# Reading the moving operand of 256-token products by turns from two halves, with u, hid and ry begun at a multiple of 1024 bytes

## The reference

```python
def _swiglu(xn, w_in, w_out):
    a, b = jnp.split(xn @ w_in, 2, axis=-1)
    return (jax.nn.silu(a) * b) @ w_out
```

## Time and profile before

| | |
|---|---|
| median of 3 runs | 2204.13 us (2203.73 to 2204.4) |
| the profiled execution's own time | 2210.91 us |
| its span, from first to last instruction | 2209.1 us |
| TensorE matmuls, busy | 2198.0 us (99%), 18114 instructions |
| TensorE weight loads, busy | 2180.8 us (99%), 18114 instructions |
| VectorE, ScalarE, GpSimd busy | 73%, 58%, 13% |
| granted TensorE clock | full in all 40 slices (2.4 GHz) |
| DMA engines | 52.2% on the queue of the weights, 174 GB/s read and written over the span |

### The profile page before, as it was taken

How to read it: one execution, slowest core, us unless ns; L and a number is a source line. 1 busy time by engine, 2 the same in 40 slices (tenths; PEclk the granted TensorE clock), 3 DMA queues, 4 the chain that set the end, 5 groups by cost and what they waited for, 6 DMA issues and landing times.

```text
span 2209.1 us, 48942 instructions
## 1 busy us (share of the span) xinstructions
PE 2198.0 (99%) x18114; PEld 2180.8 (99%) x18114; DVE 1602.4 (73%) x2450; ACT 1276.6 (58%) x1988; POOL 282.1 (13%) x328
## 2 busy tenths in 40 slices
PE   8999999999999999999999999999999999999999
PEld 8999999999999999999999999999999999999999
DVE  6655997665566579887768767888768766777775
ACT  6444786544444368766546646876556645565662
POOL 0001661100100136220020012010010010101000
PEclk9999999999999999999999999999999999999999
DMA  6555435555455544455555555355556645445553
GB/s 229 174 188 165 159 122 170 167 171 195 155 173 183 179 161 144 144 185 186 190 169 193 195 183 163 124 178 194 195 181 200 219 162 177 161 162 194 188 200 124
DMA packets 100408, 386.68 MB, mean 175 GB/s; under 512 B 11312, under 2 KB 12464, under 8 KB 100304
## 3 DMA queue, kind: packets, MB, share of 16 engines
q1 hardware_dynamic: 99648, 383.89, 52.2%
q0 software_dynamic: 368, 1.26, 0.2%
q10 hardware_dynamic: 288, 0.12, 0.0%
HBM read 384.18 MB, written 1.05 MB: 174 GB/s over the span
## 4 chain that ended last, share of the span: by engine, by line
PE 98%; ACT 1%; DVE 1%; issue 0%; DMA 0%; ACTq 0%
PE bank L387 16%; PE bank L389 15%; PE bank L388 15%; PE bank L395 15%; PE bank L396 14%; PE bank L397 14%; PE bank L759 1%; PE bank L1049 1%; PE bank L1050 1%; PE bank L1051 1%; PE bank L1096 0%; PE bank L709 0%; PE bank L740 0%; PE bank L940 0%; PE bank L943 0%; PE bank L942 0%
## 5 line engine op out<-in xcount | busy, mean ns | idle before, releaser
L412 DVE TENSOR_TENSOR wlo<-raw,whi 128x1024 fp32r<-128x1024 f32 (+1 forms) x677 | 893.3, 1322 | 177.8 <-ACT whi L405 165.4
L405 ACT ACTIVATE whi<-raw 128x1024 fp32r<-128x1024 f32 (+1 forms) x677 | 745.5, 1112 | 164.5 <-PE bank L389 117.2
L387 PE MATMUL bank<-u,whi 128*128 128x272 f32 (+1 forms) x1888 | 549.0, 291 | 7.1 <-DVE u L450 7.1
L389 PE MATMUL bank<-u,wlo 128*128 128x272 f32 (+1 forms) x1888 | 543.7, 288 | 0.0
L388 PE MATMUL bank<-u,whi 128*128 128x272 f32 (+1 forms) x1888 | 541.9, 287 | 0.0
L395 PE MATMUL bank<-u,whi 128*128 128x256 f32 x1888 | 529.2, 280 | 0.2
L397 PE MATMUL bank<-u,wlo 128*128 128x256 f32 x1888 | 527.4, 279 | 0.0
L396 PE MATMUL bank<-u,whi 128*128 128x256 f32 x1888 | 527.4, 279 | 0.0
L387 PEld LDWEIGHTS bank<-u,whi 128*128 128x128 f32 x1888 | 356.9, 189 | 8.0 <-DVE wlo L412 7.3
L388 PEld LDWEIGHTS bank<-u,whi 128*128 128x128 f32 x1888 | 357.0, 189 | 0.9 <-issue 0.2
L397 PEld LDWEIGHTS bank<-u,wlo 128*128 128x128 f32 x1888 | 357.6, 189 | 0.0
(11 more groups left out here) (332 smaller groups left out, 3448.8 us busy)
## 6 DMA issues: line engine op xcount, KB each, us to landing
raw<-w SPq DMA_DIRECT2D x552, 512.0 KB, 3.4
raw<-w SPq DMA_DIRECT2D x128, 704.0 KB, 4.1
h<-xT SPq DMA_DIRECT2D x4, 272.0 KB, 4.9
outT<-h SPq DMA_DIRECT2D x8, 128.0 KB, 4.7
consts<-cst POOLq DMA_DIRECT2D x1, 576.0 KB, 4.6
dist<-cst POOLq DMA_DIRECT2D x1, 192.0 KB, 2.7
rdist<-cst POOLq DMA_DIRECT2D x1, 192.0 KB, 3.0
sgain<-small POOLq DMA_DIRECT2D x1, 145.5 KB, 4.8
```

What stands on the lines that cost most here:

```text
L387: pe.matmul(out, w_h, x_hi, start=first, stop=False)
L389: return pe.matmul(out, w_l, x_hi, start=False, stop=last)
L405: act.activation(whi[:, n % RING, 0:COLS[n]], raw[:, n % RING, 0:COLS[n]], ACT.Copy).then_inc(hi_ready, 1)
L412: dve.tensor_tensor(wlo[:, n % RING, 0:COLS[n]], raw[:, n % RING, 0:COLS[n]], whi[:, n % RING, 0:COLS[n]], ALU.subtract).then_inc(lo_ready, 1)
```

## The change

Two things. `U_PAD`, `HID_PAD` and `RY_PAD` are each 16 elements (64 bytes) less, so that tiles of 256 tokens begin at a multiple of 1024 bytes in u, hid and ry. And the three matmuls of `split_products` no longer walk their 256 columns from first to last: both the moving operand and the output are given as a pattern of 8 x 2 x 16, in which 16 columns of the first half (64 bytes) are followed by the 16 columns of the second half that lie 512 bytes further, then the next 16 of the first half, and so on. Each column still meets the same output column, so what is computed is the same. `products` and all other matmuls keep their walk. The number and the order of the instructions on every engine are the same; only the walk of 8310 matmuls and the addresses differ.

```diff
-U_PAD, HID_PAD, RY_PAD = 112, 24, 144
+U_PAD, HID_PAD, RY_PAD = 96, 8, 128
...
+        def spread(x):
+
+            return x.rearrange("p (s m e) -> p m s e", s=2, e=16)
...
-            pe.matmul(out[:, 0:SEQ], w_h, x_hi, start=first, stop=False, skip_group_check=True)
-            pe.matmul(out[:, SEQ:2 * SEQ], w_h, x_lo, start=False, stop=last, skip_group_check=True)
-            return pe.matmul(out[:, 0:SEQ], w_l, x_hi, start=False, stop=last, skip_group_check=True)
+            hi_out, lo_out = spread(out[:, 0:SEQ]), spread(out[:, SEQ:2 * SEQ])
+            pe.matmul(hi_out, w_h, spread(x_hi), start=first, stop=False, skip_group_check=True)
+            pe.matmul(lo_out, w_h, spread(x_lo), start=False, stop=last, skip_group_check=True)
+            return pe.matmul(hi_out, w_l, spread(x_hi), start=False, stop=last, skip_group_check=True)
```

## The result

The changed kernel takes 2256.22 us in the median of four runs (2255.95 to 2256.39), the kernel before beside it 2203.95 (2203.73 to 2204.4). The ratio is 1.0237, with a 95% interval of 1.0219 to 1.0254: 52 us slower, where 46 us faster was forecast. The profiled execution has a span of 2254.6 us against 2209.1.

What follows compares the result with a forecast made beforehand. The prediction took TensorE's matmul spacing to bound the kernel. From the profiled 2210.9 us, -52 (walk) and +6 (start) gave 2165, and 6.8 us off for a slow execution gave a median of 2158 us; range 2143 to 2228.

Steps and rivals of the forecast that it cites:

- What bounds the kernel: Whole kernel: time is the number of TensorE matmuls times the spacing of their starts; waits for other engines about 2%.
- That stream and load hinder each other: Split products: x stream and next weights' load conflict in 64-byte blocks repeating every 256 bytes; spacing 116.3 ns against 106.7 streaming.
- Whoever starts in different blocks stays in different blocks: Walked matmuls: stream by turns moves as fast as the weight load, staying two blocks of four away; spacing 110 ns.
- the first term: The walk on 8310 split-product matmuls: spacing falls from 116.3 to 110 ns, -52 us (bounds -61 to +56).
- The floor: Weight load's own minimum spacing, taken as 110 ns from the retention's 128-column products starting 0.11 us apart.
- the likeliest case: Walked matmuls: conflicts gone, spacing 109 to 111.5 ns, whole kernel 2146 to 2170 us; chance 0.42.
- The step to the median: Whole kernel: profiled execution stood 6.8 us over the median of 2204.13, so its sum of 2165 became 2158 us.
- (a): Split products: only half the conflict goes, all run at the better level of 113.3 ns; 2185 us, chance 0.20.
- (c): All 256-column matmuls: walk buys nothing, lost start at 64 gives 120 ns; 2240 us, 2270 if walk worsens it; chance 0.20.
- The term for the start: 1530 unwalked matmuls on u, hid and ry: start moves from 64 to 0, +3.7 ns each, +6 us (bounds 0 to +10).
- Rival (d): PSUM output of walked matmuls: 15 jumps at one cycle each add 6.3 ns; 2210 or 2262 us, chance 0.08.

## Why the prediction was wrong

- *What bounds the kernel*: right. The time is the spacing of the matmuls, other engines stay hidden, and 45.5 us of span come out of two spacings and two counts.
- *That stream and load hinder each other*, read from one pattern in the earlier trace rows: right in that the distance between them counts, which the shifted weights show. Wrong in its shape. It was put as meetings in four kinds of 64-byte block and nothing else; the runs with one kind of block each refute that this is all, and the starts at 48 and 80 show a finer scale.
- **The step that failed** is "Whoever starts in different blocks stays in different blocks", the walk in step with the load, from which the first term took 110 ns. The walk is at 120.0 ns at the four distances tried, at one of them at 123.3 in two stages of five (mean 121.2). Jumps cost in the read of the moving operand, and the level of 113.3 ns, at which the profiled execution of before has two fifths of its split products, is lost. The term was -52 us; it measures +42, (121.2 - 116.1) x 8310, in which the new start has its part. What a jump does inside the engine stays open.
- *The floor*, 0.11 us from the earlier trace rows: the row was right and the rounding hid the point. 111.7 ns is the lowest seen, so even a walk without any conflict had (116.1 - 111.7) x 8310 = 37 us to win and not 52. From the profiled execution's 2210.9 us that leaves 2174, and the kernel with the stream held takes 2173.03: the whole of the likeliest case's own range (2146 to 2170 us) lay under it. The 109.2 ns that the Trainium skill, page "TensorE: Matmul & The Clock Gate", section "Back-to-back issue gap", gives for a matmul by itself is met by the split products of no run here.
- *The step to the median*: the forecast took its gain from the profiled execution's mix of levels, 116.3 ns at 2210.9 us, and then took 6.8 us more off because that execution was a slow one. A change that ends both levels ends that difference too, so its own sum gave 2165 us, not 2158; rivals (a) and (c), reckoned from 2204 with the same 116.3, are too low by as much. That is an error of 7 us in a miss of 98.
- *The term for the start*, +6 us on 1530 matmuls: the sign was right, 3 us measured. But the same term applies to the 8310 as well (118.7 against 116.1 with the old walk), and the forecast gave that loss only to rival (c).
- *Rival (c)*, slower by the start, came near in mechanism: 2240 us, or up to 2270 if the walk makes it worse. Of the two losses it names the one; the start alone gives 2236.5. Its mechanism for the walk (the load reads from its end) has no support: then one of the four distances should have been good. It had a chance of 0.20, and the range was cut at 2228 through its middle.
- *Rival (d)*, the output's walk: refuted, with its price of a cycle for a jump, though its 2262 us is the number nearest to the result. The price sits on the operand's side, and in the runs that compute the whole result it is 0.14 to 0.23 ns, a third to a bit over half of a cycle.

## What to carry to other kernels

A matmul stream with a load of weights for each product can run at one of several levels that the profile's page does not show; take the distance between starts, and see whether the same instruction has more than one, before reckoning with a mean. If a few per cent of TensorE matter, try the start of the moving operand against the start of the weights, in steps finer than 64 bytes, and keep the operand's walk straight: it is the jumps in the read that cost, not those in the output. And a model fitted to one pattern in a trace is worth a kernel that puts it to its extreme (here, both operands held in blocks that cannot meet, or the stream held on one column) before a change is built upon it.

## What the runs showed of the hardware

- The kernel before settles at 113.3 or 117.8 ns for a whole stage, with the same addresses, and not the same stages in every execution. A feed-forward stage with 256 tokens has 1584 matmuls, and 1584 x 4.5 ns is 7 us: that is the distance of the steps on which its runs lie (2204, 2211, 2218, 2224 us). The kernel with the weights held bears this out: its levels are 3.4 ns apart, 1584 x 3.4 ns is 5.4 us, and its eight runs lie at 2191, 2196 to 2197, 2201 to 2202 and 2207 us. What throws the choice is open; in the profiled execution of before it changes only where TensorE has waited or done other products. Kernels in which the operand is read by turns vary by less than 1 us.
- Fifteen jumps in the PSUM output of a matmul, in runs of 64 bytes, cost nothing that these runs tell (at most 0.5 ns of 118.7).
- Why a jump in the read costs 0.14 to 0.23 ns, and more for steps of 128 bytes than for returns over 512, stays open. So does what the lowest spacing of 111.7 ns consists of: 256 columns at 2.4 GHz are 106.7 ns, and no kernel here had matmuls without a load of weights beside them.
